# A two-layer decoder step: seven moves of work, and the prompt's scores in three rounded passes

## The reference

```python
y = silu(layer_norm(conv(ext) + b_dw, ln_g, ln_b)); m = y @ w_pw2 + b_pw2     # layer 0
a = einsum('bnsgd,sdh->bngh', chunks, w1[:STRIDE]); b = einsum(..., w1[STRIDE:])  # compress(k or v)
kcc = einsum('bngh,hd->bngd', silu(a[:, :-1] + b[:, 1:] + c), w2)
ls = einsum('bqgrd,bqgkld->bqgrkl', q_rot, k_selected) * scale                 # selected blocks
lw = einsum('bqgrd,bkgd->bqgrk', q_rot, k_window) * scale                      # window
out = g0 * softmax(lc) @ vcc + g1 * softmax(ls) @ v_selected + g2 * softmax(lw) @ v_window

x = x + rms_norm(m, g1)                          # every layer, after its mixer
f = square(relu(rms_norm(x, g2) @ w_ff1)) @ w_ff2; x = x + rms_norm(f, g3)
x = x + sigmoid(x @ w_ple_gate + b) * (p @ w_ple)                              # per-layer embedding
```

## Time and profile before

| | us |
|---|---|
| median of 3 runs | 1828.74 |
| lowest and highest | 1827.53, 1831.94 |
| the profiled execution, device time | 1830.59 |
| the profiled execution, span of the trace | 1828.8 |
| PE busy in the span | 1721.0 |
| DVE, ACT and POOL busy | 758.4, 618.1, 600.8 |

### The profile page before, as it was taken

The page is one execution under the profiler, slowest core; times in us unless marked ns, Lnnn a source line. Parts: engine busy times, 40 slices in busy tenths (PEclk is TensorE's granted clock), DMA queues, the critical chain, the costliest instruction groups (busy, mean ns, idle before and its releaser), DMA issues.

```text
span 1828.8 us, 31143 instructions
## 1 busy us (share of the span) xinstructions
PE 1721.0 (94%) x13303; PEld 1587.1 (87%) x13303; DVE 758.4 (41%) x1153; ACT 618.1 (34%) x972; POOL 600.8 (33%) x286
## 2 busy tenths in 40 slices
PE   6999999899999999998998878999889999999988
PEld 5997879799999999897998545556879999999978
DVE  4999933530212122455054656776161020312242
ACT  4211035432322223244222445775342231313232
POOL 4541322133334333232333003555313334343322
PEclk9998999899999999998999998999989999999999
DMA  7239603123332222121227771001212222222211
GB/s 246 93 106 143 214 19 120 70 92 139 116 115 71 92 71 91 47 93 70 82 76 248 253 247 48 2 1 48 82 47 93 70 93 75 87 92 70 93 54 68
DMA packets 61274, 180.07 MB, mean 98 GB/s; under 512 B 22850, under 2 KB 23762, under 8 KB 47250
## 3 DMA queue, kind: packets, MB, share of 16 engines
q1 hardware_dynamic: 60466, 177.18, 29.5%
q10 hardware_dynamic: 128, 0.88, 0.3%
q0 software_dynamic: 544, 0.03, 0.0%
HBM read 167.02 MB, written 16.45 MB: 100 GB/s over the span
## 4 chain that ended last, share of the span: by engine, by line
PE 84%; DVE 4%; SPq 3%; DMA 3%; ACT 2%; issue 2%; POOL 1%; ACTq 0%; DVEq 0%
PE ps L669 22%; PE ps L671 22%; PE ps L670 22%; PE ps L782 5%; PE ps L1036 2%; PE ps L1064 2%; PE ps L715 2%; PE ps L1047 2%; POOL w_lo L592 1%; DMA attn_t<-in_win 1%; SPq L536 1%; SPq L509 1%; DMA big<-v_kept 1%; PE ps L893 1%; ACT w_hi L1105 1%
## 5 line engine op out<-in xcount | busy, mean ns | idle before, releaser
L592 POOL TENSOR_TENSOR w_lo<-w_raw,w_hi 128x2048 fp32r<-128x2048 f32 x98 | 452.8, 4621 | 890.9 <-ACT w_hi L1105 890.9
L669 PE MATMUL ps<-ha,w_hi 128*128 128x288 f32 x1920 | 576.4, 300 | 29.9 <-DVE hb L1466 13.0
L670 PE MATMUL ps<-hb,w_hi 128*128 128x288 f32 x1920 | 572.5, 298 | 0.0
L671 PE MATMUL ps<-ha,w_lo 128*128 128x288 f32 x1920 | 572.1, 298 | 0.0
L669 PEld LDWEIGHTS ps<-ha,w_hi 128*128 128x128 f32 x1920 | 366.9, 191 | 37.5 <-issue 25.9
L670 PEld LDWEIGHTS ps<-hb,w_hi 128*128 128x128 f32 x1920 | 367.2, 191 | 0.0
L671 PEld LDWEIGHTS ps<-ha,w_lo 128*128 128x128 f32 x1920 | 367.1, 191 | 0.0
L669 PE MATMUL ps<-hid_hi,w_hi 128*128 128x288 f32 x1024 | 301.8, 295 | 0.0
L671 PE MATMUL ps<-hid_hi,w_lo 128*128 128x288 f32 x1024 | 301.7, 295 | 0.0
L670 PE MATMUL ps<-hid_lo,w_hi 128*128 128x288 f32 x1024 | 301.7, 295 | 0.0
L1105 ACT ACTIVATE w_hi<-w_raw 128x2048 fp32r<-128x2048 f32 x98 | 186.9, 1907 | 174.0 <-PE ps L671 165.1
(11 more groups left out here) (242 smaller groups left out, 1986.5 us busy)
## 6 DMA issues: line engine op xcount, KB each, us to landing
w_raw<-in_w SPq DMA_DIRECT2D x98, 1024.0 KB, 4.8
ring<-in_sel_pages SPq DMA_DIRECT2D x64, 256.0 KB, 4.0
ring<-in_cmp_pages SPq DMA_DIRECT2D x40, 256.0 KB, 4.5
attn_t<-in_win SPq DMA_DIRECT2D x16, 512.0 KB, 6.7
cmp_hb<-in_cmp_pages SPq DMA_DIRECT2D x16, 256.0 KB, 4.2
x<-in_x SPq DMA_DIRECT2D x4, 576.0 KB, 5.8
out_y<-x SPq DMA_DIRECT2D x8, 288.0 KB, 2.1
big<-in_cmp_pages SPq DMA_DIRECT2D x8, 256.0 KB, 4.1
```

Source lines behind the costliest of these rows:

```text
L592: nc.gpsimd.tensor_tensor(w_lo[j % 2][:, :], w_raw[:, k, :], w_hi[j % 2][:, :].bitcast(F32), ALU.subtract).then_inc(w_ready, 1)
L669: nc.tensor.matmul(to, wh, chunk(hi, k, a * HT, HT), start=k == 0, stop=False)
L670: nc.tensor.matmul(to, wh, chunk(lo, k, a * HT, HT), start=False, stop=False)
L671: return nc.tensor.matmul(to, wl, chunk(hi, k, a * HT, HT), start=False, stop=k == C - 1)
```

## The change

It makes seven moves and one replacement.

1. `UNITS` now ends with the keys of samples 5, 6, 7 and then their values; the mean goes before the last key unit, the statistics after the second last unit, the spread between the halves of the last; the last product of the compression goes into pw2's k loop (`beside`). The state stores go from behind page 1 to behind page 3. DVE makes all subtractions before the additions of squares, POOL splits pw2's second weight after its last addition.
2. ACT's split of the third block of each MLP's first `up` goes from among the hidden tiles to the end of the work on the MLP's input.
3. In `ple` PE makes its first tile before the statistics and its second before the spread. ACT makes upper parts between the copies, DVE each lower part in the loop of the sums.
4. The pairs' transfers are cut into keys and values; the keys' go right after the first block of v_tok is ready, the store of kv_cmp and the load of w1 behind them, then the values' pairs. The waits for them are cut likewise.
5. The store of k_rot goes from ahead of the first pages to behind the keys' window of sample 2.
6. In the sample loop SP loads the next sample's window of keys before its pages.
7. For n = 0 and 1 the two branches of a chunk are one pair, so `PAIRS` has 6 in place of 8 for each c.

The replacement: the prompt's scores are three passes, q_hi·k_hi, q_hi·k_lo and q_lo·k_hi, in place of one full-precision matmul. ACT makes four pieces `key_hi` and eight `query_hi`, DVE four `key_lo` and eight `query_lo` (128 × 512 each); at the loop's start two key pieces and one query piece stand ahead of the last sample's `heads_out`.

```diff
-UNITS = [(b, v) for b in range(NB - 2) for v in range(2)] + [(b, v) for v in range(2) for b in (NB - 2, NB - 1)]
+UNITS = [(b, v) for b in range(NB - 3) for v in range(2)] + [(b, v) for v in range(2) for b in range(NB - 3, NB)]
...
-            BLOCKS += [("win_k", _b)] + [("sel_pages", _b + 1)] * (_b + 1 < NB) + [("win_v", _b)]
+            BLOCKS += [(_s2, _b + 1) for _s2 in ("win_k", "sel_pages") if _b + 1 < NB] + [("win_v", _b)]
...
-PAIRS = [(c, r, n) for c in range(C) for n in range(PT) for r in range(2)]
+PAIRS = [(c, rs, n) for c in range(C) for rs, n in [((0, 1), 0), ((0, 1), 1), ((0,), 2), ((1,), 2), ((0,), 3), ((1,), 3)]]
...
+            def pair_rows(v):
+                sp.wait_ge(w_ready, W_OF["v_tok"] + v + 1)
...
-                if (src, row) == ("cmp_pages", 1):
+                if (src, row) == ("cmp_pages", 3):
                     sp.wait_ge(glu_done, 2 * C)
                     sp.dma_start(out["conv_p"], conv_in[:, :, SEQ:EXT_P]).then_inc(conv_stored, 16)
...
                 for half in range(2):
+                    if half == 1 and u == 2 * NB - 1:
+                        compress_out(u - 1)
+                        spread(1)
...
                 std(n)
+                split_weight(W_OF[f"up{layer}0"] + 2)
...
+                for p in range(3):
+                    for e in range(2):
+                        part = slice(64 * e, 64 * e + 64)
+                        qs = chunk(hid_lo, c)[part, queries] if p == 2 else q_hi[part, c % 2, queries]
...
+                        last = nc.tensor.matmul(ps[:, 2 * (i % 2) + e, 0:len(rs) * w].rearrange("p (r k) -> p r k", k=w),
+                                                qs, ks, start=p == 0, stop=p == 2)
...
+            dve.wait_ge(kept_out, 16 * 3)
+            for r in range(2):
+                key_lo(r, 0)
+            query_lo(0)
             heads_out(NB - 1)
```

More of the change, by code:

```diff
@@ L656, in block_there, with dense @@
                 pe.wait_ge(block_in[PLACE[i][1]], LOADED[i])
-            def dense(stage, norm=None):
+            def dense(stage, norm=None, beside=None):
                 name = INPUT[stage]
@@ L688, in dense @@
                         last = square_sums(mix[:, k, :], k == 0, k == C - 1)
+                    if beside is not None and k == C // 2:
+                        beside()
                 if norm is not None:
@@ L691, in dense @@
                 for m in range(2, dict((s[0], s[1]) for s in STAGES)[stage]):
+                    if m == 2 and beside is not None:
+                        pe.wait_ge(w2_out, 2 * NB)
                     if m % 2 == 0:
@@ L808, in _ @@
                 compress(u)
-                if u >= 1:
+                if 1 <= u < 2 * NB - 1:
                     compress_out(u - 1)
[L811 to L817, removed]
-                    last = nc.tensor.matmul(STAT[:, a, :], tab("mean"), src[:, a * HT:(a + 1) * HT],
-                                            start=i == 0, stop=i == len(LATE))
-            last.then_inc(mean_ready, 1)
-            for u in (2 * NB - 2, 2 * NB - 1):
-                compress(u)
-                compress_out(u - 1)
-            compress_out(2 * NB - 1)
-            stats(1)
-            spread(1)
-            dense("pw2")
+                if u == 2 * NB - 5:
+                    mean()
+                if u == 2 * NB - 2:
+                    stats(1)
+            pe.wait_ge(hid_ready, 2 * NB - 1)
+            pe.wait_ge(w2_out, 2 * NB - 1)
+            dense("pw2", beside=lambda: compress_out(2 * NB - 1))
             stats(2)
@@ L1060, in p_out @@
                 pe.wait_ge(pt_out[1], i + 1)
-                for j in range(n + 1):
+                for k, (r, j) in enumerate((r, j) for r in rs for j in range(n + 1)):
                     for e in range(2):
@@ L1600, in _ @@
             mlp(0, 4)
-            post_norm(4, 3)
-            for m in range(C):
-                lo_part("x0", m, x[:, m, :])
+            post_norm(4, 3, "x0")
             ple(0, 5)
@@ L1802, in _ @@
             mlp(1, 8)
-            post_norm(8, 7)
-            for m in range(C):
-                lo_part("x1", m, x[:, m, :])
+            post_norm(8, 7, "x1")
             ple(1)
```

260 lines of the change are left out of this document (165 added, 95 removed).

## The result

The changed kernel takes 1774.86 us in the median of 4 runs (1768.82 to 1782.07), the kernel before 1830.34 (4 runs); the ratio is 0.970, 95% interval 0.966 to 0.974. The forecast was 1776 in a range of 1761 to 1797. The profiled execution is the shortest of the four, 1768.82, with a span of 1767.0, so its stages add up to more (61.7) than the medians differ by (55.5).

A forecast was written before the change was run, and what follows sets the result against it. PE's own work, its waits and the lower clock behind them bound the kernel. Terms 12.6 + 8.7 + 9.2 + 6.5 + 6 + 10 = 53.0 off 1830.59 give 1777.6, less 1.85 to the median: 1776, range 1761 to 1797.

The forecast's parts named there:

- Compression: Compression and layer norm: waits for a page, the reciprocal root and the first lower part go; 12.6 us, bounds 10 and 14.
- The two covers of half a unit: End of compression: the last unit's halves, 3.5 us before and after the spread, each about as long as the chain beside it.
- Third weight: Each MLP's third weight: splitting it earlier removes PE's 2.8 us wait and 1.6 of low clock; both layers 8.7, bounds 7 and 9.
- Embedding: Per-layer embedding: waits before statistics and gate, and the low clock, mostly go; two layers 9.2 us, bounds 7 and 11.
- Loads ahead of the compressed scores: Before the compressed scores: the 5.4 us wait for v_kept goes, with 1.1 of clock; 6.5 us, bounds 2 and 8.
- Sample loop: Sample loop: loading the next window's keys ahead of pages gains 6 us, bounds 0 and 10.
- a third of the 18 idle us: Sample loop: the share of PE's idle time taken as the gain, giving 6 us.
- Rival 2: Sample stage and loads ahead of it: DMA holds them, so two terms give 2 us, not 12.5; 1786 us, chance 0.12.
- Prompt loop: Prompt loop: three passes and two pairs fewer cut 18.84 us a c to 17.4; gain 10 after start loss, bounds 0 and 21.
- Rival 3: Prompt loop: each pass's load hides behind the other half's matmul; scores 3.8 us a c, gain 21, 1765 us, chance 0.07.
- rival 1: Prompt loop doesn't shorten: halves take turns, or exponentials, copies and differences set the pitch; gain 0, 1786 us, chance 0.14.
- Rival 4: Prompt loop: a rounded pass with 64 rows costs the full-precision 1.64 ns a column; slower, 1851 us, chance 0.04.

## Why the prediction was right, and where it was not

The total was right, 1774.86 against 1776, and the stalls that it named went where it said. That it came so near is in part luck: in the two traces the prompt loop brought 5.5 more than forecast and the sample loop some 3 less. Point by point:

- **Compression: right, for a reason that I had only half.** 15.5 in this trace; in the mean of the twelve traces 12.5, against one trace of before, the forecast being 12.6. The two covers of half a unit held to the hundredth, so the 0.5 kept back for each wasn't needed, and page 4 was never late. Of the 1.6 kept back for pw2's first pieces 1.04 shows, in the wait at 266.09. What is late next I didn't name: with the stores away, PE is in seven of the twelve traces at the mean before DVE has done the convolution, and from the mean's second half to pw2 the rest is nearly fixed: 33.7 us in this trace, 35.7 to 36.0 where the wait was long and the clock behind it lower. That is most of the 15% of DVE on the path. The stores' part is shown by undoing it; the new places of the mean, the statistics and the spread are read from the traces alone.
- **Third weight: right**, 8.5 by the edit that undoes it, 8.7 forecast (2 × (2.8 + 1.6) is 8.8); 9.9 between the two traces.
- **Embedding: a little mis-sized, 11.2 in place of 9.2.** I kept back 1.0 a layer for the next weight's lower part; that margin held. The wait ahead of the statistics is 0.6, as estimated (0.8).
- **Loads ahead of the compressed scores: right**, 6.8 for 6.5; the wait for v_kept is gone. No run undoes this move. The stretch takes 165.7 to 167.1 in twelve of the thirteen traces that have it and 170.4 in one, the kernel with the late stores and the new order.
- **Sample loop: mis-sized, about 2.5 in place of 6**: 1.3 in the table, and 1.2 by which the wait ahead of the first prompt scores grew, where I had 1.5. (With the mean of the six loops, 87.3, the 1.3 would be 1.) The step that failed took a third of the 18 idle us as if all of them waited for transfers. In PE's waits of before, windows had 4.6; ACT and DVE inside one sample had 8.9, which no order on SP moves; and 5.9 in three waits is put down to issue. The order did what it should (5 us by undoing it), but pages became late where windows had been: 5.1 us in three waits. Rival 2 named the wrong cause: 5.5 MB less saved 2.7.
- **Prompt loop: mis-sized, 17.0 in place of 11.5.** The 1.5 lost at its start was nearly right, 1.2. Two steps failed, and both are prices of PE's own work. Taken from start to start in the timelines and less idle time, PE's work went down by 2.13 us a chunk, 17.1 in all, where I had 1.44; the loop's waits stayed, 7.7 before and 7.8 after.
  - First, the scores: 1.23 a chunk less where I had 0.84. I read 0.107 twice in a burst of two passes as a load for each pass. In the earlier trace rows a two-pass burst can't tell that from a head and a tail; the three passes can. At 512 columns they start 0.34 and 0.23 apart, then 0.32 to the next instruction, and 512 columns at 0.42 ns are 0.21: 0.13 and 0.11 at the ends, 0.02 in between. Scores are 4.7 a chunk, not 5.1. Rival 3 had the hiding right and the ends wrong; its 3.8 a chunk isn't what its formula gives, 3 × 2560 × 0.42 ns, which is 3.2.
  - Second, the two pairs fewer: 0.90 a chunk less in the other bursts where I had 0.6. I read 0.23 on top of a burst of transposes and took 0.15; measured it is 0.20 for each burst of transposes and 0.19 for each of products, and 0.12 a chunk came from the products of the compressed branch, which I had at nothing.
  - What rival 1 feared, a chain over the engines, costs 11.1 us of waits with eight pairs and three passes and 7.8 with six, a small part of the loop in both.

The price of a column, 0.42 ns, said to be that of the dense stages, was near: 0.55 at 256 and 0.89 at 512 columns make 1.33 ns for three passes, 0.44 each. (A dense pass of 288 columns takes 133 ns in the trace of before, 0.46 a column.) Rival 4 is out. That the halves run side by side was right, but the reason given for it wasn't one: four times 512 columns at 0.42 ns are 0.86, less than the burst's 1.06. It was shown only by the kernel with one half's passes ahead of the other's.

## What to carry to other kernels

Split idle time by who ends it before taking a share of it: only the waits that the edit can move count. A burst of two instructions can't show whether its constant is paid for each instruction or for each burst; find one of another length before pricing a third. And merging short items may bring more than making each of them cheaper: here merging alone brought 11.8 us and the cheaper scores alone 1.6, since each burst less saves its head and tail, and a short item covers little of the way through the other engines.

## What the runs showed of the hardware

- The halves of the rows (64 partitions each) run as two streams: in the kernel with one half's three passes ahead of the other's, both first passes start together, three matmuls out of the program's order, and the burst stays at 0.90 us.
- Reads of page numbers by SP, eight ahead of the fourth sample's pages, took from 995.08 to 1002.4, up to 0.92 us each; with the reads done ahead, and the stores late, the loop's clock stayed at 1.00 and the loop at 81.3 us, where the late stores alone had 87.2.
- The same program varied by 13 us from run to run (1768.82 to 1782.07). In the traces two stretches with unchanged code move: the compression, 134.3 to 140.9 to the end of its last unit, by its clock early on and by when the convolution ends, and the sample loop, 84.9 to 89.2. A term of 2 or 3 us in either can't be read from one trace.
